# First expert stage of a two-block model: rows of every second expert pair taken from the resident tokens by one-hot products, sums moved, last weight tiles in halves

## The reference

```
g_prob = softmax(x @ w_rg + b_rg)                 # 4 groups, the best one is taken
top_v, top_i = top_k(logits of its 8 experts, 2)  # 2 experts of 32 for each token
gate = softmax(top_v) * g_val
for each expert e: y = (silu(x_e @ w1[e]) * (x_e @ w3[e])) @ w2[e]
out[token] += gate * y                            # x_e: the rows of the tokens that chose e
```

## Time and profile before

| what | value |
|---|---|
| median of 3 executions | 2095.07 us (2094.96 to 2096.04) |
| the profiled execution's own time | 2096.56 us |
| its span | 2094.8 us |
| mean granted TensorE clock | 0.955 |
| PE / DVE / ACT busy share of the span | 90% / 47% / 15% |
| HBM traffic | 606.46 MB read, 3.28 MB written |
| first expert stage, first w1 product to last spread | 1024.5 to about 1484.4 us |

### The profile page before, as it was taken

The page is one execution under the profiler, slowest core; times in us unless marked ns, Lnnn a source line. Parts: engine busy times, 40 slices in busy tenths (PEclk is TensorE's granted clock), DMA queues, the critical chain, the costliest instruction groups (busy, mean ns, idle before and its releaser), DMA issues.

```text
span 2094.8 us, 22927 instructions
## 1 busy us (share of the span) xinstructions
PE 1892.8 (90%) x9459; PEld 1050.5 (50%) x9459; DVE 978.7 (47%) x1793; ACT 316.2 (15%) x718; POOL 30.8 (1%) x45
## 2 busy tenths in 40 slices
PE   8999999999999999999999998999999966556567
PEld 5758874555588845884633333333456522122222
DVE  5538888466378895646522322322565410111111
ACT  2221110226211103011300000000235200000000
POOL 0000000000000000000100000000000000000000
PEclk9999999999999999999999999999999987787779
DMA  8458886451278864421899999999821899999998
GB/s 324 153 194 276 283 284 222 148 186 42 82 268 294 285 234 168 136 110 71 319 424 427 426 427 427 426 427 425 297 92 75 325 427 426 426 426 426 427 426 337
DMA packets 148602, 607.30 MB, mean 290 GB/s; under 512 B 14312, under 2 KB 65192, under 8 KB 124049
## 3 DMA queue, kind: packets, MB, share of 16 engines
q1 hardware_dynamic: 144224, 595.90, 72.7%
q0 software_dynamic: 4176, 9.81, 1.3%
q10 hardware_dynamic: 96, 0.10, 0.0%
HBM read 606.46 MB, written 3.28 MB: 291 GB/s over the span
## 4 chain that ended last, share of the span: by engine, by line
PE 78%; DMA 15%; DVE 2%; issue 2%; ACT 1%; SPq 1%; DVEq 0%
PE psum L2848 15%; PE psum L1185 15%; PE psum L552 9%; PE psum L2883 7%; DMA ring<-in_w 6%; PE psum L1125 6%; PE psum L2001 4%; DMA arena<-in_w 4%; PE psum L2943 4%; DMA consts<-in_w 3%; PE psum L2088 2%; PE psum L612 2%; DMA normed_t<-in_w 1%; PE psum L691 1%; PE psum L1475 1%
## 5 line engine op out<-in xcount | busy, mean ns | idle before, releaser
L1185 PE MATMUL psum<-normed_t,ring 128*128 128x256 f32 x1408 | 306.4, 380 | 0.0
L1185 PEld LDWEIGHTS psum<-normed_t,ring 128*128 128x128 f32 x1408 | 266.9, 190 | 43.5 <-issue 7.2
L2848 PE MATMUL psum<-ring,arena 128*32 128x512 f32 (+1 forms) x752 | 234.3, 667 | 56.9 <-DMA normed_t<-in_w 17.8
L1037 DVE SCALAR_TENSOR_TENSOR arena<-ring,silu_c,arena 128x1024 f32<-128x1024 f32 x168 | 204.7, 1279 | 0.0
L552 PE MATMUL psum<-ring,normed_t 128*128 128x512 f32 x448 | 198.1, 599 | 3.6 <-DVE resid L3341 1.5
L2848 PE MATMUL psum<-consts,arena 128*32 128x512 f32 (+1 forms) x288 | 147.0, 668 | 23.6 <-DMA ring<-in_w 19.0
L3341 DVE TENSOR_TENSOR resid<-resid,psum 128x512 f32<-128x512 f32 x128 | 79.6, 682 | 178.1 <-PE psum L2943 178.1
L2848 PE MATMUL psum<-arena 128*32 128x512 f32 (+1 forms) x300 | 114.4, 668 | 32.2 <-DMA arena<-in_w 19.7
L552 PEld LDWEIGHTS psum<-ring,normed_t 128*128 128x128 f32 x448 | 84.5, 192 | 106.3 <-issue 105.3
L2848 PEld LDWEIGHTS psum<-ring,arena 128*32 128x32 f32 (+1 forms) x752 | 64.2, 131 | 146.4 <-issue 146.4
L3356 DVE TENSOR_TENSOR scaled<-scaled,psum 128x512 f32<-128x512 f32 x24 | 16.5, 688 | 202.1 <-PE psum L2848 202.1
(11 more groups left out here) (613 smaller groups left out, 2876.4 us busy)
## 6 DMA issues: line engine op xcount, KB each, us to landing
ring<-in_w SPq DMA_DIRECT2D x90, 2048.0 KB, 32.2
arena<-in_w SPq DMA_DIRECT2D x36, 2048.0 KB, 31.7
consts<-in_w SPq DMA_DIRECT2D x26, 2048.0 KB, 33.3
ring<-in_w_mod SPq DMA_DIRECT2D x24, 2048.0 KB, 7.9
ring<-in_ffn_w_up SPq DMA_DIRECT2D x44, 1024.0 KB, 7.7
normed_t<-in_w SPq DMA_DIRECT2D x18, 2048.0 KB, 30.7
ring<-in_ffn_w_down SPq DMA_DIRECT2D x10, 2048.0 KB, 7.8
ring<-in_ab_w_in SPq DMA_DIRECT2D x6, 2048.0 KB, 15.7
```

What stands on the lines that cost most here:

```text
L1037: ins = dv.scalar_tensor_tensor(out=acc, in0=w, scalar=sc, in1=acc, op0=ALU.mult, op1=ALU.add)
L1185: m = pe.matmul(PS[:, b, 256 * hf:256 * hf + 256], w[:, hf, k, P * cc:P * cc + P], HT[:, k, 0:T], start=(k == 0), stop=(k == KC - 1))
L2848: m = pe.matmul(PS[r, 2 + q, :], self.XT[c % 2][k // 4][:, k % 4, r], self.weights(c, q, h, FE * k, FE), start=k == 0, stop=k == KC - 1)
```

## The change

For even pairs (`on_chip`) the rows no longer come by indirect DMA. The new `pe_first(c)` makes them, not turned, in banks 6 and 7: 16 matmuls with a 32-column one-hot block of `SEL` stationary and 512 columns of `XM` moving. ACT copies them to `FIRST_ROWS`, and `pe_turn` transposes them, in `pe_out(c-1)` between the hidden transposes and the w2 product; `act_xt` of such a pair comes after `hgt`. This holds for pair 0 too, in place of `pe_select(0)`. Odd pairs (`picked_up`) are still gathered. `XM` now stays whole, so `XG` and `XT` have one buffer each. `SEL` of a later pair is made on DVE at the start of the pair before. `spread(c-1, 0)` moves ahead of `pe_hidden(c, 0)`, `spread(c-1, 1)` from `pe_out(c)` to behind `pe_hidden(c, 0)`, with other banks, and all eight additions come before `prod`. The last six groups of tiles (pairs 14 and 15) are loaded in halves, and their products wait for the second half midway. The diff, cut to its core:

```diff
-        XG = Z[:, 0:2048].rearrange("p (b n) -> p b n", b=2)
+        XG = GB[:, 1, :]
+        FIRST_ROWS = CST[:, AB_DEAD + 1024:AB_DEAD + 2048]
...
-                self.XT = [[four(v[:, 0:512]), four(v[:, 512:1024])] for v in (self.turned, Z[:, 3072:4096])]
+                self.XT = [[four(v[:, 0:512]), four(v[:, 512:1024])] for v in [self.turned] * 2]
...
+                self.on_chip = [c for c in range(self.groups) if nt == 2 or c % 2 == 0]
+                self.picked_up = [c for c in range(self.groups) if c not in self.on_chip]
...
+            def second_half(self, c, q):
+                i = 3 * (c - self.groups) + q + self.halved
+                return self.second_halves[i] if i >= 0 else None
+
+            def load_halves(self, sp, c, q):
+                for half in range(2):
+                    for h in range(self.lanes):
+                        n = self.tile(c, q, h)
+                        if half == 0:
+                            sp.wait_ge(sems["pe"], upto("pe", self.done_with(n - self.ns)))
+                        cols = slice(2048 * half, 2048 * half + 2048)
+                        sp.dma_start(self.slots[n % self.ns][0][:, cols], self.source(n)[:, cols])\
+                            .then_inc(self.second_half(c, q) if half else self.w_loaded[n % self.ns], 16)
...
+            def pe_first(self, te, c):
+                pe, p, L = te.eng, te.p, self.L
+                pe.wait_ge(sems["dve"], upto("dve", f"{L}.sel.{c}"))
+                if c >= 2:
+                    pe.wait_ge(sems["dve"], upto("dve", f"{L}.add13.{c - 2}"))
+                for hf in range(2):
+                    if c == 0:
+                        wait(pe, *te.banks[6 + hf])
+                    for j in range(2):
+                        for q in range(4):
+                            t = 2 * (q % 2) + j
+                            m = pe.matmul(PS[ROOM * q:ROOM * q + ROOM, 6 + hf, :], self.SEL[c][:, t, q // 2, :], XM[:, t, 512 * hf:512 * hf + 512],
+                                          start=j == 0, stop=j == 1)
+                    p.step(m, f"{L}.first{hf}.{c}")
...
# pe_turn
+                rows_of = FIRST_ROWS if c in self.on_chip else XG
                 for hf in range(2):
+                    if c in self.on_chip:
+                        pe.wait_ge(sems["act"], upto("act", f"{L}.rows{hf}.{c}"))
...
# pe_hidden
+                    if k == 4 and self.second_half(c, q):
+                        pe.wait_ge(self.second_half(c, q), 16 * self.lanes)
...
# pe_out, behind the hidden transposes
-                if c >= 1 and not ending:
-                    if self.nt == 4:
-                        self.pe_spread(te, c - 1, 1)
+                if self.nt == 4 and c + 1 in self.on_chip:
+                    self.pe_turn(te, c + 1)
...
# pe_spread, waits and banks
-                return ((5, 0, 4, 1), (5, 3, 2, 0))[n][t]
+                return ((5, 0, 4, 1), (6, 5, 7, 4))[n][t]
-                if n == 1 and c < self.groups - 1:
+                if n == 0 and c < self.groups - 1:
+                    pe.wait_ge(sems["act"], upto("act", f"{L}.xt0.{c + 1}"))
+                    pe.wait_ge(sems["dve"], upto("dve", f"{L}.xt1.{c + 1}"))
+                elif c < self.groups - 1:
+                    pe.wait_ge(sems["dve"], upto("dve", f"{L}.add02.{c}"))
                     pe.wait_ge(sems["dve"], upto("dve", f"{L}.add00.{c}"))
...
# pe, the loop over pairs
-                self.pe_select(te, 0)
+                if nt == 4:
+                    self.pe_first(te, 0)
+                self.pe_turn(te, 0)
...
                 for c in range(self.groups):
+                    if c >= 1 and self.nt == 4:
+                        self.pe_spread(te, c - 1, 0)
                     self.pe_hidden(te, c, 0, lists if c == 0 else None)
                     ...
                     elif c >= 1:
-                        self.pe_spread(te, c - 1, 0)
+                        self.pe_spread(te, c - 1, 1)
                     ...
                     self.pe_hidden(te, c, 1)
-                    if c + 1 < self.groups:
+                    if self.nt == 4 and c + 1 in self.on_chip:
+                        self.pe_first(te, c + 1)
+                    elif c + 1 < self.groups:
                         self.pe_turn(te, c + 1)
...
# act: rows_of(c + 1) behind silu.c, act_xt(c + 1) behind hgt.c, for even c + 1
+                def rows_of(c):
+                    for hf in range(2):
+                        ac.wait_ge(sems["pe"], upto("pe", f"{L}.first{hf}.{c}"))
+                        p.step(ac.activation(FIRST_ROWS[:, 512 * hf:512 * hf + 512], PS[:, 6 + hf, :], ACT.Copy), f"{L}.rows{hf}.{c}")
...
# pool
-                for c in range(1, self.groups):
-                    po.wait_ge(sems["pe"], upto("pe", f"{L}.turn1.{max(c - 2, 0)}"))
+                for i, c in enumerate(self.picked_up):
+                    if i:
+                        po.wait_ge(sems["pe"], upto("pe", f"{L}.turn1.{self.picked_up[i - 1]}"))
```

More of the change, by code:

```diff
@@ L2602, in __init__ @@
                 self.over_row_made = s("over_row_made")
-                self.last_parts = [s(f"last_part{i}_loaded") for i in range(1 if nt == 4 else 2)]
-                self.rows_in = [s(f"rows_in{b}") for b in range(2)]
+                self.last_parts = [s(f"last_part{i}_loaded") for i in range(2)] if nt == 2 else []
+                self.halved = 6 if nt == 4 else 0
+                self.second_halves = [s(f"second_half{i}_loaded") for i in range(self.halved)]
+                self.rows_in = s("rows_in")
                 self.units = [(t, n) for g in range(nt // 2) for n in range(2) for t in (2 * g, 2 * g + 1)]
@@ L2651, in __init__ @@
                 self.CT = R[:, 400:400 + 32 * (nt + self.halves)].rearrange("p (t e) -> p t e", e=NE)
-                first_at = R[:, 592:600] if nt == 4 else DEAD[:, 3520:3584]
+                first_at = PRM[:, 306:434] if nt == 4 else DEAD[:, 3520:3584]
                 self.FIRST = first_at.rearrange("p (c t h) -> p c t h", t=nt, h=self.lanes)
@@ L2658, in __init__ @@
                 one_hot = lambda v: v.rearrange("p (t h r) -> p t h r", t=nt, h=self.lanes)
-                self.SEL = [one_hot(XSF[:, 1280:1280 + P * nt])] + ([one_hot(SM[:, 256:512])] * (self.groups - 1) if nt == 2 else [])
+                later = SM[:, 256:512] if nt == 2 else XSF[:, 512:768]
+                self.SEL = [one_hot(XSF[:, 1280:1536])] + [one_hot(later)] * (self.groups - 1)
+                self.on_chip = [c for c in range(self.groups) if nt == 2 or c % 2 == 0]
+                self.picked_up = [c for c in range(self.groups) if c not in self.on_chip]
                 self.TM = SM[:, 256:256 + 64 * nt].rearrange("p (t k e) -> p t k e", t=nt, k=2)
@@ L2733, in load_weights @@
                 src = self.source(n)
-                if n >= self.tiles - self.lanes:
+                if n >= self.tiles - self.lanes and self.nt == 2:
                     view, of = self.last_part(n, 0)
@@ L2770, in sp @@
                             self.load_early(sp, n, part)
-                for n in range(self.ns + 4, self.tiles):
+                for n in range(self.ns + 4, self.tiles - self.lanes * self.halved):
                     self.load_weights(sp, n)
+                for i in range(self.halved):
+                    self.load_halves(sp, self.groups - 2 + i // 3, i % 3)
                 self.load_last_parts(sp)
@@ L2802, in pe_turn @@
             def pe_turn(self, te, c):
-                pe, p, L, b = te.eng, te.p, self.L, c % 2
+                pe, p, L = te.eng, te.p, self.L
                 if self.nt == 2:
                     pe.wait_ge(sems["dve"], upto("dve", f"{L}.sel.{c}"))
-                else:
-                    pe.wait_ge(self.rows_in[b], 16 * (c // 2) + 16 * b)
+                elif c in self.picked_up:
+                    pe.wait_ge(self.rows_in, 16 * (self.picked_up.index(c) + 1))
                 if c >= 1:
@@ L2840, in pe_hidden @@
                     wait(pe, *(("act", f"{L}.silu.{c - 1}") if q == 0 else ("dve", f"{L}.prod.{c - 1}")))
-                if c >= 2 and q == 0 and self.nt == 4:
-                    pe.wait_ge(sems["dve"], upto("dve", f"{L}.add13.{c - 2}"))
                 for k in range(KC):
@@ L2866, in pe_out @@
                 p.step(m, f"{L}.hidt.{c}")
-                if c >= 1 and not ending:
-                    if self.nt == 4:
-                        self.pe_spread(te, c - 1, 1)
-                    else:
-                        self.pe_combine(te, c - 1, (2, 3))
+                if self.nt == 4 and c + 1 in self.on_chip:
+                    self.pe_turn(te, c + 1)
+                if c >= 1 and not ending and self.nt == 2:
+                    self.pe_combine(te, c - 1, (2, 3))
                 if ending:
@@ L2895, in pe_out @@
                     product(1, (2, 3))
-                elif last:
+                elif self.second_half(c, 2):
                     for n in range(2):
                         product(n, (0, 1))
```

(41 more changed lines are left out.)

6 lines of the change are left out of this document (1 added, 5 removed).

## The result

The changed kernel takes 2106.82 us (median of four executions, 2104.14 to 2109.79) against 2095.56 before: ratio 1.0048, 95% interval 1.0033 to 1.0063, 10 us slower by the ratio. Timed again beside the experiments it gives 1.0057 (1.0041 to 1.0073). The forecast was slower by 5.8 us, 2100.9; the median lies 0.8 us over the top of the stated range of 2088 to 2106; by the ratio on the 2095.07 of the forecast it is 2105.1, just under it. The profiled execution took 2105.24 us (span 2103.3) against 2096.56, 8.7 more.

A forecast was written before the change was run, and what follows sets the result against it. Weights bound the first expert stage from pair 8, PE earlier; after the change PE throughout. Terms -22.0 + 24.5 + 5.6 - 2.4 + 0.1 = +5.8 us on 2095.07 gave 2100.9 us, range 2088 to 2106.

The forecast's parts named there:

- Which line decides: First expert stage: PE's own work, not weight loading, bounds every pair after the change, ending 22.0 us of waits and slower clock.
- PE's line: First expert stage timed by PE's work alone: 27.17 us a pair before the change, a mean of 29.32 after.
- over 10: Sign, end of the first expert stage: the last weight tiles land over 10 us before PE uses them.
- The waits before a w1 product: Sign, pairs 8 to 14: PE's waits for weights vanish; with slower clock they cost 22.0 us before.
- `pe_first`: Term, seven even pairs after pair 0: new row matmuls on PE cost 3.5 us each, +24.5 us.
- The moved spread: Term, pairs 2, 4, ... 14: `hgt` uncovered before the w2 product, 0.8 us each, +5.6 us.
- Start: Term, pair 0: the new row step takes 4.96 us in place of 7.38, -2.4 us.
- End: Term, pair 15 to the end of its last product: 27.85 us against 27.77, +0.1 us.
- A: Rival, first expert stage: weights stay the bound and added PE work fills waits; -11.4 us, 2083.7; chance 0.12.
- C: Rival, no change: `hgt` gap 0.6, `pe_first` 3.44, start -3.0; +3.4 us, 2098.5; chance 0.20.
- B: Rival, `pe_first`: column groups don't run four abreast, 7.02 us a call; 2129; decides from 2.8 a call; chance 0.04.
- D: Rival, first expert stage: two to four dips of PE's granted clock cost +3 to +6 us, 2104 to 2107; chance 0.09.

The follow-up runs named there:

- e1: Changed kernel with half of the one-hot matmuls of `pe_first`, 4 rounds instead of 8; 2093.56 us, ratio 0.9984 to the kernel before.
- e10: Changed kernel with every one-hot matmul of `pe_first` done twice, 16 rounds instead of 8; 2135.25 us (one execution).
- e6: Changed kernel with whole weight tiles for pairs 14 and 15, only the last w2 tiles in halves; 2106.32 us, ratio 1.0050 to the kernel before.
- e7: Changed kernel with on-chip rows only for pairs 0, 10, 12, 14 and spreads moved only in pairs 9, 11, 13; 2092.16 us, ratio 0.9978.
- e2: Changed kernel with both spreads back in their old places in pairs whose next pair is gathered; 2094.95 us, ratio 0.9992 to the kernel before.
- e5: The changed kernel itself, timed and profiled again beside the experiments; 2106.26 us, ratio 1.0057 to the kernel before.
- e4: Kernel before with only the last six groups of tiles loaded in halves and products waiting midway; 2095.41 us, ratio 0.9994.

## Why the prediction was right, and too low

- **Which line decides: right.** PE's line holds the whole stage; e1 and e10 show it from both sides, e6 by the halves, and the last weights are there 15.8 us early, for the "over 10" of the forecast. The waits before a w1 product are gone. They were worth 22.1 us: the 15 periods before sum to 430.11, without waits 14 x 27.16 + 27.78 = 408.0.
- **`pe_first`: right.** 3.57 us and transposes 0.01 longer, for 3.5. 7 x 0.08 = 0.6 us low.
- **The moved spread: the term that failed.** I charged 0.8 for the uncovered `hgt` in seven pairs, 5.6 us. It is 0.89 there, and I wrote that "the spreads themselves cost the same wherever they stand". They do, but the products beside them don't: 0.15 + 0.07 in all 14 pairs, 3.1 us, and the gap is 0.6 larger over the seven. I had applied the Trainium skill's rule (TensorEngine Tiling (Array Packing), section Tiling Modes: changing the tiling mode drains the engine) to `pe_first` alone, and not to the spread that now splits a run of products. By that rule, and by 6.87 against 7.02, the 0.15 was there to be read in the earlier trace rows.
- **Start: right** (-2.3 for -2.4). **End:** +0.5 for +0.1, the same three small costs in pair 15.
- **Sum.** 7 x 3.83 (26.8) + 7 x 1.11 (7.8) + 0.5 - 22.1 - 2.3 = +10.7, the measured stage. Against the forecast: 0.6 from `pe_first`, 3.7 from the moved spreads, 0.4 from the end, 0.2 of rounding.
- **Rivals.** A needed the added work to lie in waits; the stage had them only from pair 8 on, and the added work came from pair 1. e7 shows A true where the work is put late. C is out: the gap is 0.89 for its 0.6, `pe_first` 3.57 for 3.44, the start -2.3 for -3.0. By the sum's own terms B's break-even is (22.0 + 2.4 - 0.1 - 5.6) / 7 = 2.7 us a call, and not 2.8; this changes nothing. D did not happen: in the changed kernel, e1, e2, e5, e6 and e10, which have no wait for weights, the granted clock is 1.00 through the stage; what dips there are stand in kernels that wait, and e7 waits and has none.

## What to carry to other kernels

Where two resources are both full, find the lead of one over the other and what each gives up per step; a saving on one is capped by the waits it ends, and its price on the other is paid from the first step at which that one decides. Put such a trade only into the steps that wait. When an operation is moved between two matmul groups, count the separate runs of one form before and after, and what it covered where it stood.

## What the runs showed of the hardware

- The stage bound by PE repeats to 0.1 us in three profiles (473.62 to 473.70). The code ahead of it does not: in the thirteen profiles the stage begins between 1012.5 and 1019.5. How far the stage repeats when loads bound it is not shown, since no kernel of that kind was profiled twice.
- Issuing a load on SP can take longer than 0.43 us. In e4 most issues of 1 MB take 2.1 us or more from the point where nine or more loads are issued and not landed (some 24 us of transfers). In the kernel before, with up to eight such loads, an issue of the stage's weights takes mostly 0.33 or 0.43 us, with as much as 32 us of transfers queued. So it is not the amount of data that is queued; the cause was not tried.
- 128 rows by 32 columns, four groups with four different moving tensors: 8 rounds in 3.57 us, 16 in 7.00, so 3.43 for each eight and 0.14 once (e10); the four rounds of e1 take 1.85, which fits.
